# Second attention with stationary values, two heads at once, and the value projection's chunks in between

## What is computed

```python
proj = h @ w_in                                   # dq dk dv mq mk mv, 512 columns each
out_a = differential_attention(dq, dk, dv, ...)   # first attention, 4 heads of 2 maps
s = where(kpos <= qpos, q @ k.T * scale, -inf)    # second attention ("MoBA"), 8 heads of 64:
out_b = softmax(s) @ v                            # with 256 tokens there is one block, so it is plain causal
h = layer_norm(ALPHA * h + concat(out_a, out_b) @ w_out)
k, v = split(layer_norm(mem) @ w_kv)              # memory keys and values
h = layer_norm(ALPHA * h + softmax(q(h) @ k.T) @ v @ w_o)
h = layer_norm(ALPHA * h + moe(h))                # 32 experts, top 4, all their weights are read
```

## Time and profile before

| | |
|---|---|
| median of 3 executions | 1188.84 us (1185.05 to 1189.12) |
| the profiled execution | 1189.85 us, its span 1188.0 us |
| busy: TensorE, VectorE, ScalarE | 92%, 27%, 22% of the span |
| read from HBM | 444 MB, 375 GB/s over the span |
| mean granted TensorE clock | 0.979 of full |

### The profile page before, as it was taken

The page is one execution under the profiler, slowest core; times in us unless marked ns, Lnnn a source line. Parts: engine busy times, 40 slices in busy tenths (PEclk is TensorE's granted clock), DMA queues, the critical chain, the costliest instruction groups (busy, mean ns, idle before and its releaser), DMA issues.

```text
span 1188.0 us, 16129 instructions
## 1 busy us (share of the span) xinstructions
PE 1094.0 (92%) x6597; PEld 534.0 (45%) x6597; DVE 321.6 (27%) x726; ACT 255.7 (22%) x416; POOL 9.1 (1%) x14
## 2 busy tenths in 40 slices
PE   7999999999999999999999988888888888888895
PEld 5788899883333333343333333333333333333331
DVE  4986576553111111221111111111111111111114
ACT  3575645412111111111111111111111111111110
POOL 0000000000000000000000000000000000000000
PEclk9999799979999999999999999999999999999998
DMA  8756487578899999999999999999999999999994
GB/s 283 278 172 229 148 289 251 213 283 328 370 426 429 427 429 428 429 428 429 429 428 429 429 429 428 430 427 429 429 428 429 428 429 428 429 429 428 427 428 169
DMA packets 49597, 445.64 MB, mean 375 GB/s; under 512 B 5536, under 2 KB 6176, under 8 KB 24896
## 3 DMA queue, kind: packets, MB, share of 16 engines
q1 hardware_dynamic: 49568, 445.23, 91.0%
HBM read 444.16 MB, written 1.05 MB: 375 GB/s over the span
## 4 chain that ended last, share of the span: by engine, by line
PE 61%; DMA 22%; SPq 7%; DVE 4%; ACT 4%; issue 1%; another core or an unknown queue 1%; POOL 0%; DVEq 0%; ACTq 0%
PE bank L904 25%; DMA ring<-in_w_mlp 21%; PE bank L933 13%; SPq L435 6%; PE bank L546 3%; PE bank L548 3%; PE bank L547 3%; PE bank L845 3%; PE bank L836 3%; DMA w_raw<-in_w_in 1%; DVE w_low L1214 1%; ACT live L1185 1%; ACT live L1154 1%; PE bank L892 1%
## 5 line engine op out<-in xcount | busy, mean ns | idle before, releaser
L904 PE MATMUL bank<-ring,live 128*64 128x512 f32 x2048 | 458.4, 598 | 41.6 <-DMA ring<-in_w_mlp 41.6
L904 PEld LDWEIGHTS bank<-ring,live 128*64 128x64 f32 x2048 | 143.0, 137 | 338.2 <-issue 247.4
L933 PE MATMUL bank<-ring,live 128*64 128x512 f32 x1024 | 230.2, 603 | 22.0 <-ACT live L1185 22.0
L1582 DVE TENSOR_SCALAR live<-bank 128x256 f32<-128x256 f32 x64 | 24.2, 420 | 739.8 <-PE bank L904 739.8
L933 PEld LDWEIGHTS bank<-ring,live 128*64 128x64 f32 x1024 | 71.5, 138 | 158.6 <-issue 130.5
L1181 ACT ACTIVATE live<-live 128x512 f32<-128x512 f32 x32 | 20.1, 629 | 463.2 <-DVE live L1582 463.2
L1214 DVE TENSOR_TENSOR w_low<-w_raw,w_high 128x1024 fp32r<-128x1024 f32 x64 | 75.4, 1220 | 25.3 <-ACT w_high L997 25.1
L997 ACT ACTIVATE w_high<-w_raw 128x1024 fp32r<-128x1024 f32 x64 | 65.4, 1056 | 33.8 <-DMA w_raw<-in_w_in 15.9
L1187 ACT ACTIVATE live<-bank 128x512 f32<-128x512 f32 x32 | 19.1, 597 | 233.4 <-PE bank L933 233.4
L845 PE MATMUL bank<-live 64*128 64x512 f32 x256 | 63.6, 615 | 0.7 <-ACT live L1187 0.7
L836 PEld LDWEIGHTS bank<-pick,live 128*128 128x128 bf16 x1536 | 46.7, 98 | 23.6 <-issue 23.5
(11 more groups left out here) (197 smaller groups left out, 874.2 us busy)
## 6 DMA issues: line engine op xcount, KB each, us to landing
ring<-in_w_mlp SPq DMA_DIRECT2D x192, 2048.0 KB, 48.1
w_raw<-in_w_in SPq DMA_DIRECT2D x24, 512.0 KB, 8.4
w_raw<-in_w_mem_kv SPq DMA_DIRECT2D x16, 512.0 KB, 4.2
w_raw<-in_w_mix_out SPq DMA_DIRECT2D x8, 512.0 KB, 5.8
w_raw<-in_w_mem_q SPq DMA_DIRECT2D x8, 512.0 KB, 4.1
w_raw<-in_w_mem_o SPq DMA_DIRECT2D x8, 512.0 KB, 4.8
h<-in_x SPq DMA_DIRECT2D x4, 256.0 KB, 5.3
mem_o<-in_mem SPq DMA_DIRECT2D x2, 512.0 KB, 8.8
```

The lines of the kernel that those rows point to most:

```text
L904: mm = pe.matmul(up[n][64 * g:64 * g + SLOTS, :], x_e[:, k, :], slot(at)[:, col:col + 512], start=False, stop=(k == KC - 1))
L933: mm = pe.matmul(ty[64 * g:64 * g + SLOTS, :], hidT[:, P * c + 64 * u:P * c + 64 * u + SLOTS], slot(at)[:, D * c + 512 * g:D * c + 512 * ( ...
```

## The change

It does five things.

1. **Scores earlier.** Block 6 is cut in two: chunks 0 to 3, then `S` 8 to 15, then chunks 4 to 7. `vm` 0 holds its two banks all that time, so `S` 8 to 15 share six banks.
2. **Probabilities are scaled, not results.** VectorE's `norm_group` multiplies the exponentials of a group of four heads by the reciprocals before they are turned. `turn_probs` waits for that.
3. **`weigh_pair`** takes the place of `weigh` for the second attention: 64 columns of `v` stationary, 128 columns of turned probabilities streamed, head 2p into PSUM partitions 0 to 63 and head 2p+1 into 64 to 127. The results come out turned: the second half of `oT` and the copies into `mem_o` fall away, and ScalarE (`split_heads`) and VectorE (`low_part`) read them straight into block 8's operand.
4. **Block 7 in pieces** between the heads: chunks 0, 1; then 2; then 3; 4; 5, 6; 7.
5. **`cs`** moves behind `S` 0 to 7 on TensorE and behind `mask_group(1)` on VectorE, and the banks are planned anew, always the longest unused of those allowed.

```diff
@@ plan_banks @@
+    def take(names, allowed=range(8)):
+        for name in names:
+            b = next(b for b in by_age if b in allowed)
+            by_age.remove(b)
+            by_age.append(b)
+            plan[name] = (b, used[b])
+            used[b] += 1
...
+    take(tiles("dk") + tiles("dv") + tiles("Tdq") + tiles("Tdk"))
+    take([("memT", t, q) for t in range(NT) for q in range(2)])
+    take([("S", m) for m in range(8)] + [("cs",)])
+    take(tiles("mq") + tiles("mk") + tiles("mv"))
...
+    take(tiles("Tmq") + tiles("Tmk") + tiles("vm", 0))
+    take([("S", m) for m in range(8, 16)], without(tiles("vm", 0)))
+    take(tiles("vm", 1), without(tiles("vm", 0)))
+    free = without(tiles("vm", 1))
+    take([("TA", 4), ("oT", 0, 0), ("oT", 1, 0), ("TA", 5), ("TA", 6)], free)
+    for p in range(4):
+        take([("PVT", p)] + [("TA", j) for j in (2 * p + 7, 2 * p + 8) if j < 12], free)
+    take(tiles("mix", 0) + tiles("mix", 1))
@@ TensorE @@
+            def weigh_pair(p):
+                b = bank_for(pe, "PVT", p)
+                heads = [2 * p, 2 * p + 1]
+                for hd in heads:
+                    wait_drained(pe, "TA", 4 + hd)
+                for key, n, probs in ((0, 0, 0), (0, 1, 1), (1, 1, 2)):
+                    for i, hd in enumerate(heads):
+                        mm = pe.matmul(b[HD * i:HD * (i + 1), P * n:P * (n + 1)], v[:, key, 512 + HD * hd:512 + HD * (hd + 1)],
+                                       aT[:, hd % GROUP, P * probs:P * (probs + 1)], start=(probs < 2), stop=(probs != 1))
+                mm.then_inc(filled_by("PVT", p), 1)
...
-            project_rows(6, left_m, (("vm", 0, 0), ("vm", 0, 1)), turned_rows("memT"))
+            project_rows(6, left_m, (("vm", 0, 0), ("vm", 0, 1)), turned_rows("memT"), chunks=range(4))
...
             for m in range(8, 16, 2):
                 score_pair(m)
-            project_rows(7, left_m, (("vm", 1, 0), ("vm", 1, 1)))
+            project_rows(6, left_m, (("vm", 0, 0), ("vm", 0, 1)), turned_rows("memT"), chunks=range(4, KC))
...
+            values([0, 1])
             for t in range(NT):
                 wait_drained(pe, "mv", t)
             turn_probs(4)
             pe.wait_ge(o_ready, 1)
             for t in range(NT):
                 turn_rows("oT", mem_o, t, 0)
-            for j in range(4, 12):
-                if j < 11:
-                    turn_probs(j + 1)
-                weigh(j)
-            pe.wait_ge(o_ready, 2)
-            for t in range(NT):
-                turn_rows("oT", mem_o, t, 1)
+            turn_probs(5)
+            turn_probs(6)
+            values([2])
+            for p in range(4):
+                weigh_pair(p)
+                for j in (2 * p + 7, 2 * p + 8):
+                    if j < 12:
+                        turn_probs(j)
+                values([[3], [4], [5, 6], [7]][p])
@@ ScalarE @@
+            exps(2)
             copy_vm(0)
-            exps(2)
             exps(3)
             split(2)
             copy_probs(4)
             split_rows("oT", left, BY_HALF[0:NT])
+            copy_probs(5)
+            copy_probs(6)
+            split(1)
+            for p in range(4):
+                for j in (2 * p + 7, 2 * p + 8):
+                    if j < 12:
+                        copy_probs(j)
+                split_heads(p)
+                if p == 1:
+                    split(1)
             copy_vm(1)
@@ VectorE @@
+            def norm_group(g):
+                invert(g)
+                for i in range(GROUP):
+                    for t, at in enumerate((slice(0, P), slice(P, SEG))):
+                        last = dve.tensor_scalar(scores[:, g % 2, i, at], scores[:, g % 2, i, at],
+                                                 recips[:, g, t, i:i + 1], None, ALU.mult)
+                last.then_inc(mixed, 1)
...
             split(4)
             mask_group(2)
             mask_group(3)
+            norm_group(2)
             split(2)
+            norm_group(3)
             split_rows("oT", left, BY_HALF[0:NT])
-            invert(2)
-            invert(3)
-            for j in range(8):
...
+            split(1)
+            for p in range(4):
+                b = wait_filled(dve, "PVT", p)
+                low_part(left[:, 1, 4 + p, :], b[:, 0:S], left[:, 0, 4 + p, :], "PVT", p)
+                if p == 1:
+                    split(1)
```

More of the change, by code:

```diff
@@ L103, in plan_banks @@
 def plan_banks():
[L105 to L140, removed]
+    plan, used, by_age = {}, [0] * 8, list(range(8))
+    def take(names, allowed=range(8)):
[5 more added lines that the diff above has]
+            used[b] += 1
@@ new lines, in tiles, with without @@
+    def tiles(*name):
+        return [name + (t,) for t in range(NT)]
+    def without(names):
+        return [b for b in range(8) if b not in [plan[name][0] for name in names]]
+    take([("xT", t, 0) for t in range(NT)] + tiles("dq") + [("xT", t, 1) for t in range(NT)])
+    take(tiles("dk") + tiles("dv") + tiles("Tdq") + tiles("Tdk"))
+    take([("memT", t, q) for t in range(NT) for q in range(2)])
+    take([("S", m) for m in range(8)] + [("cs",)])
+    take(tiles("mq") + tiles("mk") + tiles("mv"))
@@ new lines, in plan_banks @@
+    take([("TA", 0), ("TA", 1), ("PV", 0), ("TA", 2), ("PV", 1), ("TA", 3), ("PV", 2), ("PV", 3)])
+    take(tiles("Tmq") + tiles("Tmk") + tiles("vm", 0))
[5 more added lines that the diff above has]
+        take([("PVT", p)] + [("TA", j) for j in (2 * p + 7, 2 * p + 8) if j < 12], free)
@@ new lines, in plan_banks @@
+    take(tiles("mix", 0) + tiles("mix", 1))
+    take([("kmT", 0, j) for j in range(4)])
+    take([("h1T", t, q) for t in range(NT) for q in range(2)])
+    take([("kmT", 1, j) for j in range(4)])
+    take([("qmT", 0, j) for j in range(4)] + [("MS", 0), ("MS", 1)])
+    take([("qmT", 1, j) for j in range(4)] + [("TP", 0), ("TP", 1), ("MS", 2), ("MS", 3)])
+    take([("PM", 0), ("TP", 2), ("PM", 1), ("TP", 3), ("PM", 2), ("PM", 3)])
+    take(tiles("mo", 0))
+    take(tiles("mo", 1), range(4, 8))
@@ L141, in plan_banks @@
+    for name, b in ((("rT", 0, 0), 0), (("rT", 1, 0), 1), (("rT", 0, 1), 2), (("rT", 1, 1), 3), (("lg", 0), 0), (("lg", 1), 1),
+                    (("rank", 0), 2), (("rank", 1), 2)):
+        take([name], [b])
     for b, (t, g) in enumerate((t, g) for t in range(NT) for g in range(2)):
@@ L408, in free_slot @@
                 elif at == 3:
-                    wait_filled(sp, "PV", 11)
+                    wait_filled(sp, "PVT", 3)
                 elif at == 4:
@@ L551, in weights, with project_rows @@
                 return [w_high[:, (u + 2) % SPLIT, c % 2, cols], w_low[:, u % RAW, c % 2, cols]]
-            def project_rows(blk, act_, names, before=None, by_tile=False, between=None):
+            def project_rows(blk, act_, names, before=None, by_tile=False, between=None, chunks=range(KC)):
                 b = [bank_for(pe, *names[t]) for t in range(NT)]
                 for tiles in ([[0], [1]] if by_tile else [[0, 1]]):
-                    for c in range(KC):
+                    for c in chunks:
                         u = UNITS * blk + c // 2
@@ L631, in weigh @@
                 b = bank_for(pe, "PV", j)
[L632 to L637, removed]
-                    .then_inc(filled_by("PV", j), 1)
+                at = aT[:, j, :]
+                pe.matmul(b[:, 0:P], at[:, 0:P], v[:, 0, P * j:P * (j + 1)], start=True, stop=True)
+                pe.matmul(b[:, P:2 * P], at[:, P:2 * P], v[:, 0, P * j:P * (j + 1)], start=True, stop=False)
+                pe.matmul(b[:, P:2 * P], at[:, 2 * P:3 * P], v[:, 1, P * j:P * (j + 1)], start=False, stop=True)\
+                    .then_inc(filled_by("PV", j), 1)
+            def weigh_pair(p):
[8 more added lines that the diff above has]
+                mm.then_inc(filled_by("PVT", p), 1)
             def turn_x(q):
@@ L652, in _ @@
                 project_rows(i, left, ((kind, 0), (kind, 1)), other_half_of_x if i == 0 else None)
[L653 to L657, removed]
             turn_heads("dq", 0)
@@ L668, in _ @@
                 score_pair(m)
+            b = bank_for(pe, "cs")
+            pe.wait_ge(sums_ready, 1)
+            pe.matmul(b[:, 0:2 * E], router_b[:, 0:P // E, :].rearrange("p c n -> p (c n)"),
+                      router_sums[:, :, :].rearrange("p a n -> p (a n)"), start=True, stop=True)\
+                .then_inc(filled_by("cs"), 1)
             project_rows(3, left, (("mq", 0), ("mq", 1)))
@@ L686, in _, with values @@
                 score_pair(m)
-            project_rows(7, left_m, (("vm", 1, 0), ("vm", 1, 1)))
+            project_rows(6, left_m, (("vm", 0, 0), ("vm", 0, 1)), turned_rows("memT"), chunks=range(4, KC))
+            def values(chunks):
+                project_rows(7, left_m, (("vm", 1, 0), ("vm", 1, 1)), chunks=chunks)
+            values([0, 1])
             for t in range(NT):
@@ L1102, in _ @@
             split_rows("oT", left, BY_HALF[0:NT])
-            copy_vm(1)
```

(7 more changed lines are left out.)

30 lines of the change are left out of this document (14 added, 16 removed).

## The result

| | before | after |
|---|---|---|
| median | 1185.23 us (1181.22 to 1189.9, 7 runs) | 1194.12 us (1191.0 to 1197.51, 7 runs) |
| the profiled execution | 1189.85 us | 1194.85 us, its span 1193.1 us |
| ratio after/before | | 1.0061, interval 1.0041 to 1.008 |

By the ratio the change costs 7.2 us (4.9 to 9.5), 0.6%; the two medians are 8.9 us apart. The forecast was 1.3 us. The time lies in the forecast range and just under the 1194.8 us from which the forecast counted "slower", but the ratio is above the 0.5% that it called "no change".

The account below looks back on a forecast made before the run. The end hangs on when the experts' loop starts, behind a VectorE and ScalarE chain; block 8 at 144.2 - 0.9 = 143.3 against 141.95 made 1.3 us, so 1188.84 + 1.3 = 1190.1 us, range 1184 to 1196.

Parts of the forecast that it names:

- The four waits: TensorE idle before `S` 14 (6.55 us), the first pair (3.2), head 8 (1.3) and block 8 (1.4), 12.45 in all.
- the waits are not there: Rival, second attention: masks start before 110 us, TensorE runs through; 1175.5 us, or 1182 with half the waits; chance 0.11.
- The clock after the waits: TensorE at half clock for 3.2 us after a restart: 1.2 us lost after `S` 14's wait, 0.9 after head 5's.
- half until block 8: Rival: clock stays at half from head 5's wait until block 8, 9 us more than the sum, 1199 us; chance 0.09.
- a clock of 0.5 after 133 us: Sign of a wrong forecast: TensorE's granted clock at 0.5 later than 133 us.
- The weighting by pairs: Second attention's `weigh_pair` on TensorE: 0.65 us a pair with halves overlapping, plus 0.5 for eight changes of tiling.
- The whole stretch: TensorE's work, waits, clock losses and tiling changes up to block 8, which would start at 144.2 us before `cs`'s gain.
- within 2 us of 142: Sign of a right forecast: block 8 on TensorE starts within 2 us of 142.
- The base: Kernel before: block 8 starts at 141.28 us plus 0.67 for its slow start, 141.95; median 1188.84 us.
- the gain on offer: Stretch of the second attention, without any wait at full clock: 6.1 us in place of 17.8 + 0.67, 12.4 gained.
- The move of `cs`: Block 3 on TensorE starts at 58.0 instead of 58.95 us: 0.9 gained (0.4 to 1.1).
- Later loads and the banks' plan: SyncE's loads of units 34 to 39 and place 2 come 10 to 17 us later, at no price.

Follow-up runs that it names:

- e2_masks_first: Kernel after with VectorE's list reordered: mask_group(2) ahead of the splits, which follow one by one; 1184.51 us, ratio 0.9971.
- a_again: The kernel after, unchanged, profiled once more; 1194.28 us in one execution.
- e4_cs_only: Kernel before with only `cs` moved behind `S` 0 to 7; 1184.28 us in one execution.
- b_again_1: The kernel before, unchanged, profiled once more; 1182.55 us in one execution.
- e1_scores_after_block6: Kernel after with block 6 whole again ahead of the scores and ScalarE's copy of `vm` 0 ahead of both exponentials; 1187.75 us, ratio 0.9998.
- e5_interleave_repaired: Kernel after with both masks ahead of three of four splits and block 7's chunks in other portions; 1183.48 us, ratio 0.9958.
- e6_other_banks: Kernel after with block 8's first tile on banks other than `vm` 1's; 1192.06 us in one execution.
- e3_pair_only: Kernel before with only the weighting changed to pairs, ScalarE copying heads 5 and 6 ahead of `vm` 1; 1181.11 us, ratio 0.9944.
- e7_pair_and_masks: Kernel before with weighting by pairs and, in VectorE's list, the first mask ahead of two of four splits; 1181.36 us, ratio 0.9942.

## Why the forecast was right about the waits and wrong about the size

**The four waits: right.** Forecast 6.55, 3.2, 1.3 and 1.4 us; measured 6.4, 1.9, 1.1 and 0.7. The order, the releaser and the engine of each are as forecast. The first is VectorE's order of work (`e2_masks_first` takes it away without touching TensorE). The second came out shorter because TensorE itself came later to it, slowed by the clock: it was ready at 128.2 instead of 124.6, ScalarE's copy at 130.1 instead of 127.8. The rival "the waits are not there" falls with this: the masks began at 112.01, not before 110.

**The clock after the waits: right in kind, too small.** I counted 3.2 us at half after a restart, 1.2 of it felt, and 0.9 after the second wait. The trace has 5.3 us at 0.50 after `S` 14, which loses 2.7, and 3.5 us at 0.52 around the third, which loses at most 1.7. `a_again` shows them again, half the clock from 109 to 114.6 and from 128.8 to 135.5. The rival "half until block 8" did not come true: the last 10.5 us ran at 1.00. But the text also named a clock of 0.5 after 133 us as a sign of being wrong, and that one came, until 135.5.

**The weighting by pairs: right in kind.** A pair's twelve records were forecast as 0.65 a pair plus 0.09 for each change of tiling. From the first pair's start to the transposes behind it go 0.81 (130.13 to 130.94), and from the last to the chunk behind it 0.81 (142.83 to 143.64). Halves that do not overlap would be 1.39. The Trainium skill, page TensorEngine Tiling, section Key Properties, says that a change of tiling mode drains the engine; with a whole record each, a pair would stand 1.04 from what follows. The trace does not show that, so a change here costs at most 0.16 (0.81 less the forecast's 0.65), in the order of the 0.09 of the forecast.

**The whole stretch: nearly right.** From 96.55 to the forecast's 144.2 go 47.7 us; measured 48.8 and 49.1. The waits were 2.3 us shorter than forecast (10.1 against 12.45) and the clock's losses 2.2 us larger (4.3 against 2.1), which cancels. The missing 1.2 to 1.5 lies in the work between them, such as 0.3 in the four pairs; the rest I have not broken down. Block 8 itself started at 146.03, not within 2 us of 142, the text's sign of being right: to this 1.2 come 0.6 us by which this execution was late at the mq heads already, and the 0.9 that the move of `cs` did not bring.

**The base: one of two lengths, which the forecast did not know.** It compared with "141.28 + 0.67 = 141.95", a stretch of 44.7 us with the clock at half from 128.8 into block 8. That half clock is a property of some executions and not of the kernel: 44.7 and 44.3 in two, 39.8 in the third and also in `e4_cs_only`, which has the same attention. Against the short one, the change costs 9.1 to 9.4 us of stretch, against the long one 4.1 to 4.8. With block 8's slow start counted in, from the mq heads to the experts' loop, it is 172.3 us in both profiles of the kernel after, 168.5 in both long ones of before and 163.0 in the short one and in `e4_cs_only`: 3.8 or 9.3 us. So of the 12.4 us that the forecast valued as the gain on offer "at full clock", the kernel before has 5.5 by itself whenever its clock holds. As a median, though, the base of 1188.84 us was sound: the 55 later runs have 1188.75. That the seven runs of the result have 1185.23 is nothing that the forecast could have summed up, and 3.5 us of the 8.9 between the two medians are that. What the weighting by pairs, with its order of copies, truly saves of full-clock stretch is 39.8 - 37.7 = 2.1 us, from one profile of each; beyond that it spares the executions that fall to half, at least in the one profile of it, where the clock stayed at 1.00.

**The move of `cs`: wrong by 0.9.** The forecast counted 0.9 us gained. Block 3 of the kernel after started at 58.80 and not at 58.0, against 58.95. Counted from the last matmul of block 2, at full clock, block 3 starts at 9.8 in the unchanged kernel and at 9.9 in `e4_cs_only`. VectorE's draining of `memT`, 1.6 and 0.3 us of wait, took the place of the 2.46. The profiled execution of after also has a piece at half clock there, around 58 to 60 us, so its mq heads come 48.9 us behind block 2, against 48.7 before. I had set a forecast at full clock against a row at half, the same mistake in small.

**Later loads and the banks' plan: right,** nothing of them is seen beyond the 0.7 us.

**The sum, and its terms that failed.** The forecast added 2.2 us for the stretch (144.2 less 141.95), -0.9 for `cs` and nothing behind block 8. Against the long base that it used, the runs show 3.8, some 0.1 and 1.2, together 5.1: near the 5.0 between the two profiled executions and the 5.4 from the 55 runs' median. So the work of the stretch was mis-sized by 1.5, the gain by `cs` was not there, and "what stands behind block 8 on all queues is unchanged" was no reason for a zero. Against the short base the sum is 10.6; the measured 7.2 lies between. The 1.2 us is in TensorE's last rows of the kernel after:

```profile
1179.31 1.12 PE L872 MATMUL bank<-live 64*128 64x512 f32 x3 [0.70 <-ACT live L1225]
1181.37 1.44 PE L872 MATMUL bank<-live 64*128 64x512 f32 x5 [0.94 <-issue]
```

and in those of `b_again_1`, where the eight run together:

```profile
1167.93 1.99 PE L845 MATMUL bank<-live 64*128 64x512 f32 x8 [0.70 <-ACT live L1187]
```

The gap stands in every kernel with the changed weighting (1.41 us in `a_again`, 1.64 in `e1_scores_after_block6`, 1.30 in `e2_masks_first`, 1.47 in `e5_interleave_repaired`, 1.29 in `e6_other_banks`, but only 0.37 and 0.19 in `e3_pair_only` and `e7_pair_and_masks`), and in none of the four profiles with the old one. It waits for nothing that the profile shows; what makes it was not tried and stays open. Here I take the mean of the gaps of the two profiles of after, 0.94 and 1.41.

Such things also part `e5_interleave_repaired` from `e3_pair_only`, which have the same stretch. Their medians are 2.4 us apart, the two profiled executions 5.4. Of these, 2.3 lie ahead of the stretch (mq heads at 97.86 and 95.58; only the first execution has a piece at half clock, around 58 to 61 us), 1.1 are the gap, and 1.7 the last expert's matmuls, 8.78 us against 7.09:

```profile
1159.75 8.78 PE L960 MATMUL bank<-ring,live 128*64 128x512 f32 x32 [0.69 <-ACT live L1224]
...
1171.82 1.44 PE L872 MATMUL bank<-live 64*128 64x512 f32 x5 [1.47 <-issue]
```

and in `e3_pair_only`:

```profile
1157.54 7.09 PE L947 MATMUL bank<-ring,live 128*64 128x512 f32 x32 [0.69 <-ACT live L1210]
...
1167.68 1.01 PE L859 MATMUL bank<-live 64*128 64x512 f32 x2 [0.37 <-issue]
```

The 1.7 us are no property of the interleaving: the kernel before has 8.78 us in two of its profiles, 7.09 in the third. How much of the medians' 2.4 us each part explains is not shown.

**The best version** is `e3_pair_only`, level with `e7_pair_and_masks`: the weighting by pairs without the interleaving, 0.994 of the kernel before.

## What to carry to other kernels

Before a profiled execution serves as the base of a sum, look where it lies in the spread of the kernel's runs and whether a stretch of it ran at half the clock; if so, profile the kernel again and work the sum out against both levels. And do not read a few microseconds out of few runs: seven runs of one kernel had a median 3.5 us under that of 55 others. Moving work ahead on one engine brings nothing as long as the consumer's list has other work in front of it, and a PSUM bank kept occupied meanwhile turns the unused lead into a wait: first reorder the consumer (here worth 8.8 us), then move the producer. Put pieces of a block between other work only where a wait exists that they fill.

## What the runs showed of the hardware that was not expected

- **The clock's fall is not settled by the program.** Behind the same wait of 1.1 us the same kernel was granted 1.00 in one profile and 0.50 in two from 128.8 to 139.6 us, and the stretch was 39.8 or 44.3 to 44.7 us.
- **An issue gap that comes and goes with the program.** The last eight sums, the same in all kernels, run without a gap in four profiles with the old weighting and with 0.19 to 1.64 us of issue time in the eight with the new one, a thousand microseconds behind the changed part.
- **A 64-column stationary operand in f32 at 128 columns.** Twelve records in the two halves of PSUM take 0.81 us from start to start, the change behind them included; the experts' rate at 512 columns, scaled by the columns, gave 0.65.
